# Norms of two halves of the tokens among the products, up weights in the ring's last words, and another fill at the recurrence's end

## The chip, the cores and the metric

The kernel runs on one core of a Trainium2 chip. The metric is the device time of one execution in microseconds (us), as the median of several runs. All data is fp32. A matmul instruction of the program is executed in fp32 as two passes, so that the trace counts 16 records where the program has 8 instructions. "PE" is the matmul engine, "PEld" its weight loads, DVE the vector engine, ACT the scalar engine, POOL the GpSimd engine, SP the engine that issues most transfers.

## The reference, cut to what matters

512 tokens of width 1024 are worked on: 256 of the context and 256 of the latent. Two blocks follow each other.

```
# first block: two layers
h = rmsnorm(x, norm_pre[i]) * (1 + scale) + shift          # both sequences
y = hgrn2_mixer(h) (i = 0) or mla_mixer(h) (i = 1)         # ends in @ w_out, 2048 -> 1024
x = x + gate * rmsnorm(y, norm_post[i])                    # layer 1: latent only
# second block: two layers
h = modulate(rms_norm(x, norm_mix[l]), sh1, sc1)
k, v, q, u, f, gt = split(h @ w_in[l])
x = x + g1 * merge_branches(attention, pool, fourier, gt) @ w_out
hf = modulate(rms_norm(x, norm_ffn[l]), sh2, sc2)
x = x + g2 * conv_ffn(hf, w_up[l], conv_w[l], w_down[l])
```

The context of the second block is a new input (`ctx_2`); its latent part is what the first block gives. The norm's mean goes over the width of one token, so the norm of one token never needs another token.

## The kernel before

Activations lie transposed: the width on the 128 partitions in 8 parts `k`, the tokens along the row, columns 0 to 255 the context (`CTX`), 256 to 511 the latent. `xT` is the stream, `hT` the normed input of a layer, `oz` the 16 heads of the recurrence, `ozm` those of the latent attention. All engines run programs written by hand and meet only at semaphores; the order on each engine is the order of the code.

**Weights** come through `ring_mem`, 12288 words for each partition, cut anew for each stage (`ring.stage`): slot `j` of a stage lies at `j * words`. SP runs one `ring.fill` after another in program order; before it loads a slot it waits until the last stage's user of these words (or of this slot's semaphore) is done (`strips_used`). `out{l}` has four slots of 2048 words, `up{l}` two slots of 2048 with 11 turns, `down{l}` four slots of 2816 words with two turns. So slots 0 and 1 of `up` (words 0 to 4095) lie where slots 0 and 1 of `down` (words 0 to 5631) will lie.

**A norm** (`norm_scalar`, `norm_tensor`, `norm_vector`) takes 8 squares on ACT, 8 matmuls with a matrix of ones that sum them over the partitions into a PSUM bank (L370), a root on ACT (L362), a reciprocal on DVE (L375), 8 products on DVE (L383), and where the layer modulates, 8 or 16 activations on ACT with scale and shift (L436, L444), which raise `h_ready` for the next matmuls. `post_vector` multiplies a mixer's output by the reciprocal (L1677) and adds it with its gate to `xT` (L1683).

**The recurrence** works on 8 pairs of heads (`PAIRS`). For a pair there are seven terms: PE forms scores (L703), DVE multiplies decays into `Kw`, `Qw`, `Tw` (L1622, L1624, L1629) and merges scores under a mask (L1627), ACT copies keys for the next term (L1344). After the last pair has been projected nothing but these terms is left, since pair 7 cannot overlap a pair 8. There the kernel puts matmuls of `hg_out` (L1279: heads `k` below `EARLY` = 14 of strips 0 and 1) among the terms, four after each of the first seven steps; the first of them waits until pair 6 has been read out by DVE (`hg_root_vector`, `hg_read_vector`, ending at L1670). For pair 7 DVE does both reciprocals and the readout of pair 6 right behind term 1.

**Then** `outer_tensor` (L781) forms the output product in 8 strips of 128 rows on all 512 columns, the norm `hg_post`, the norm `mla_pre` and the products of `mla_in_tensor` (L800, L807) follow each other, and `mla_z` (L816). After the attention pairs, `outer_tensor` forms `mla_out` for the latent, the norms `mla_post` and `mix0` follow, and then `in_tensor` (L955 keys, L962 values, L979 queries, L1001 the other inputs). The second block's later norms (`ffn0`, `mix1`, ...) are already done in two parts of the tokens, `_a` and `_b`, each beside products of the other.

## Time and profile before

| | us |
|---|---|
| median of 3 runs | 2774.67 |
| the 3 runs | 2774.24 to 2776.05 |
| the profiled execution | 2774.83 |
| its span, first to last instruction | 2773.0 |
| PE busy in the span | 2630.5 (95%) |
| DVE busy | 902.2 (33%) |
| ACT busy | 607.2 (22%) |

The profile comes from one execution. Busy time of PE includes matmuls at the lower clock; the time lost is therefore both in its waits and in stretches in which the granted clock is below 1. A row of the timeline gives start, duration, engine, line, operation, operands, the count of merged records and, in brackets, the idle time ahead and who ended it.

### The profile page before, as it was taken

What the parts mean: (1) busy time and instruction counts of PE and PEld (TensorE: products, weight loads), DVE (VectorE), ACT (ScalarE), POOL (GpSimd) and SP (SyncE); (2) the same over time, 40 slices, a digit from 0 to 9 for tenths busy, and PEclk for the clock granted to TensorE, in tenths of its full rate; (3) what the DMA queues carried; (4) which work ended last, traced back from release to release, by engine and by line L of the source; (5) the groups of instructions that cost most, each with busy time, mean ns of one, the idle gap of its engine ahead of it and who ended that gap; (6) DMA issues with size and microseconds to landing.
All of it is one profiled execution on the core that took longest, in us unless ns stands there. A gap on an engine that the chain in (4) does not pass through costs nothing.

```text
span 2773.0 us, 29216 instructions
## 1 busy us (share of the span) xinstructions
PE 2630.5 (95%) x11486; PEld 1715.6 (62%) x11486; DVE 902.2 (33%) x1503; ACT 607.2 (22%) x1072; POOL 52.9 (2%) x42
## 2 busy tenths in 40 slices
PE   7999999999997887899889999999998999999989
PEld 4566666666665434666746444774443587889878
DVE  2236446446446212244116101123232014113321
ACT  3112212212221112233114100122221013113321
POOL 0000000000000100000000000000000000000000
PEclk9999999999998998999989999999999999999999
DMA  8443333333340312212510121222224322253562
GB/s 319 163 137 130 127 136 128 129 136 127 130 133 4 114 30 91 59 38 71 137 46 16 49 72 61 76 61 76 76 76 114 83 51 87 87 156 107 152 181 76
DMA packets 319711, 280.21 MB, mean 101 GB/s; under 512 B 27617, under 2 KB 298601, under 8 KB 319513
## 3 DMA queue, kind: packets, MB, share of 16 engines
q1 hardware_dynamic: 317882, 274.89, 32.3%
q0 software_dynamic: 1280, 4.20, 0.4%
q8 instruction: 51, 0.84, 0.1%
q10 hardware_dynamic: 479, 0.13, 0.0%
q14 instruction: 19, 0.16, 0.0%
HBM read 278.15 MB, written 1.05 MB: 101 GB/s over the span
## 4 chain that ended last, share of the span: by engine, by line
PE 93%; DVE 3%; DMA 1%; ACT 1%; issue 1%; SPq 0%; ACTq 0%; DVEq 0%
PE ps L656 16%; PE ps L1176 15%; PE ps L1099 9%; PE ps L781 5%; PE ps L1192 4%; PE ps L1202 4%; PE ps L665 4%; PE ps L703 4%; PE ps L1135 3%; PE ps L1111 3%; PE ps L423 2%; PE ps L816 2%; PE ps L370 2%; PE ps L1001 1%; PE ps L979 1%; PE ps L1162 1%
## 5 line engine op out<-in xcount | busy, mean ns | idle before, releaser
L656 PE MATMUL ps<-hT,ring_mem 128*128 128x512 f32 x1024 | 455.9, 599 | 1.7 <-ACT hT L436 1.7
L1176 PE MATMUL ps<-hT,ring_mem 128*128 128x512 f32 (+1 forms) x1280 | 414.9, 487 | 2.6 <-DMA ring_mem<-in_w_up_dram 2.6
L1176 PEld LDWEIGHTS ps<-hT,ring_mem 128*128 128x128 f32 x1280 | 244.3, 191 | 172.4 <-issue 155.4
L656 PEld LDWEIGHTS ps<-hT,ring_mem 128*128 128x128 f32 x1024 | 191.3, 191 | 235.1 <-issue 232.4
L1099 PE MATMUL ps<-hT,ring_mem 128*128 128x512 f32 (+1 forms) x768 | 250.3, 486 | 0.0
L1099 PEld LDWEIGHTS ps<-hT,ring_mem 128*128 128x128 f32 x768 | 145.9, 190 | 101.3 <-issue 91.4
L1892 DVE SCALAR_TENSOR_TENSOR arena<-ps,vecs,arena 128x510 f32<-128x510 f32 (+1 forms) x176 | 100.3, 611 | 306.3 <-ACT arena L1498 299.9
L781 PE MATMUL ps<-arena,ring_mem 128*128 128x256 f32 (+1 forms) x456 | 144.6, 480 | 7.8 <-DVE arena L1670 7.8
L1192 PE MATMUL ps<-arena,ring_mem 128*128 128x512 f32 (+1 forms) x352 | 117.2, 496 | 14.4 <-DMA ring_mem<-in_w_down_dram 14.4
L703 PEld LDWEIGHTS ps<-arena,K_c 128*128 128x128 f32 x896 | 115.2, 192 | 23.6 <-issue 23.0
L781 PEld LDWEIGHTS ps<-arena,ring_mem 128*128 128x128 f32 x456 | 87.6, 192 | 64.5 <-issue 48.5
L1855 DVE TENSOR_TENSOR arena<-ps,arena 128x512 f32<-128x512 f32 (+1 forms) x48 | 26.8, 558 | 291.2 <-PE ps L1111 291.2
L703 PE MATMUL ps<-arena,K_c 128*128 128x128 f32 x896 | 117.8, 285 | 0.0
L1202 PE MATMUL ps<-arena,ring_mem 128*128 128x256 f32 (+1 forms) x704 | 116.1, 327 | 0.0
L665 PE MATMUL ps<-ring_mem,hT 128*128 128x256 f32 x512 | 113.0, 379 | 0.0
L1202 PEld LDWEIGHTS ps<-arena,ring_mem 128*128 128x128 f32 x704 | 106.5, 191 | 9.6 <-issue 0.5
L375 DVE RECIPROCAL rstd<-root 128x256 f32<-128x256 f32 (+2 forms) x15 | 31.1, 2073 | 240.0 <-ACT root L362 240.0
L1192 PEld LDWEIGHTS ps<-arena,ring_mem 128*128 128x128 f32 x352 | 68.5, 195 | 63.1 <-issue 42.5
L1864 DVE SCALAR_TENSOR_TENSOR xT<-ps,mod_b,xT 128x256 f32<-128x256 f32 (+1 forms) x60 | 23.8, 427 | 247.9 <-PE ps L1192 115.4
L1344 ACT ACTIVATE K_c<-arena 128x1024 f32<-128x1024 f32 x56 | 64.0, 1144 | 181.8 <-DVE arena L1624 159.3
L665 PEld LDWEIGHTS ps<-ring_mem,hT 128*128 128x128 f32 x512 | 96.1, 190 | 12.4
L357 ACT ACTIVATE hT<-xT 128x256 f32<-128x256 f32 (+2 forms) x88 | 34.5, 430 | 294.5 <-DVE xT L1864 264.9
(238 smaller groups left out, 2969.6 us busy)
## 6 DMA issues: line engine op xcount, KB each, us to landing
ring_mem<-in_w_mod_dram SPq DMA_DIRECT2D x24, 2048.0 KB, 7.7
ring_mem<-in_w_up_dram SPq DMA_DIRECT2D x88, 512.0 KB, 4.5
ring_mem<-in_hg_w_in_dram SPq DMA_DIRECT2D x40, 1024.0 KB, 5.1
ring_mem<-in_w_in_dram SPq DMA_DIRECT2D x30, 1024.0 KB, 5.4
ring_mem<-in_w_down_dram SPq DMA_DIRECT2D x16, 1408.0 KB, 7.2
ring_mem<-in_ada_w_dram SPq DMA_DIRECT2D x8, 2048.0 KB, 7.7
ring_mem<-in_mla_w_in_dram SPq DMA_DIRECT2D x9, 1024.0 KB, 5.4
ring_mem<-in_hg_w_out_dram SPq DMA_DIRECT2D x8, 1024.0 KB, 11.7
```

Source lines behind the costliest of these rows:

```text
L656: mm = PE.matmul(bank, wj[:, k, m * 128:m * 128 + 128], hT[:, k, :], start=k == 0, stop=k == 7)
L665: mm = PE.matmul(bank[:, g * 256:g * 256 + 256], hT[:, k, tok:tok + 128], wj[:, k, :], start=k == 0, stop=k == 7)
L703: mm = PE.matmul(dst, K_c[:, u * 128:u * 128 + 128], comb(Qw, 1 << (term - 1), u), start=True, stop=True)
L781: mm = PE.matmul(ps[:, j, 0:n], wj[:, k, :], src(k), start=k == 0, stop=k == kts - 1)
L1099: mm = PE.matmul(ps[:, j, 0:n], wj[:, k, m * 128:m * 128 + 128], hT[:, k, c0:T], start=k == 0, stop=k == 7)
L1111: mm = PE.matmul(ps[:, 3 + j, 0:n], wj[:, k, m * 128:m * 128 + 128], brT[:, k, c0:T], start=k == k0, stop=k == k1 - 1)
L1135: mm = PE.matmul(ps[:, (0 if part == "_a" else 4) + j, m * (hi - lo):(m + 1) * (hi - lo)], wj[:, k, m * 128:m * 128 + 128], yT[:, k, c0 + ...
L1176: mm = PE.matmul(ps[:, 2 * j + m, 0:n], wj[:, k, m * 128:m * 128 + 128], hT[:, k, c0:T], start=k == 0, stop=k == 7)
L1192: mm = PE.matmul(ps[:, 4 + j, 0:n], wj[:, k, :], hid[:, k, 0:n], start=k == 0, stop=k == FT - 1)
L1202: mm = PE.matmul(ps[:, (0 if part == "_a" else 4) + j, 0:hi - lo], wj[:, k, :], hid[:, k, lo:hi], start=k == 0, stop=k == FT - 1)
L1344: S.activation(view(K_c, (2 * h, PC // (2 * h)), (h, 2), (1, h)), comb(Kw, h), ACT.Copy).then_inc(kc_ready, 1)
L1892: ins = V.scalar_tensor_tensor(dst, src, tap(k, f, part), dst, ALU.mult, ALU.add)
```

## The change

Three things change.

- **Norms in two halves.** `hg_post`, `mla_pre` and `mix0` become `_a` (context) and `_b` (latent). The second four strips of `hg_out` are formed first for the context (`h == 0`, banks 4 to 7), then for the latent (banks 0 to 3); the context's post norm and pre norm are summed in the middle of the latter. The keys' weights are used first on the context while the latent's norms run, then the queries' weights, then the keys' weights on the latent. The norm of the new context (`mix0_a`) is summed during `mla_out`; `mla_post` and `mix0_b` are summed while `in0` works on the context. Squares go to other places (`y_sq`, `z_sq`), gates have their own `coef_post`, and each norm its own bank. `post_vector` alternates its two operations.
- **Ring.** `up{l}` gets slots 4 and 5 at words 8192 to 12287.
- **Recurrence's end.** 6 fill matmuls come ahead of the first scores (they need heads 0 to 11 only), then 4, 4, 4, 4, 2, 0, 2, 2, 0 behind the steps, and the 14 heads of strip 2 behind the last. DVE does the reciprocals of pair 6 behind terms 1 and 2 and its readout behind term 3.

```diff
-            ring.stage(f"up{l}", 2, 2048, FT // 2, [2] * 2)
+            ring.stage(f"up{l}", 2, 2048, FT // 2, [2] * 2, first_slot=4, at=8192)
...
+        def hg_close_tensor(pe, done, ready):
+            for j in range(4):
+                ring.wait_loaded(pe, "hg_out", j, 0)
+                k0 = done if j < 3 else 0
+                for k in range(k0, 16):
+                    if j == 0:
+                        ready(k)
+                    mm = PE.matmul(ps[:, j, :], strip("hg_out", j, 16)[:, k, :], oz[:, k, :], start=k == 0, stop=k == 15)
+                strip_used(mm)
+            for h in range(2):
+                for j in range(4):
+                    ring.wait_loaded(pe, "hg_out", j, 1)
+                    if h == 1:
+                        pe.wait_ge(y_kept, j + 1)
+                    for k in range(16):
+                        if h == 1 and j == 0 and k == 8:
+                            pe.wait_ge(y_kept, 5)
+                            norm_tensor(pe, "hg_post_a", lambda k: y_sq[:, k, 0:CTX], ones, CTX)
...
+                    if j == 2:
+                        pe.wait_ge(y_kept, 6)
+                        norm_tensor(pe, "mla_pre_a", lambda k: hT[:, k, 0:CTX], ones, CTX)
...
+        def mla_close_tensor(pe):
+            for t in range(2):
+                for j in range(4):
...
+                    if t == 1 and j == 0:
+                        pe.wait_ge(y_kept, 13)
+                        norm_tensor(pe, "mix0_a", lambda k: hT[:, k, 0:CTX], ones, CTX)
...
         def mla_in_tensor(pe):
...
+            pe.wait_ge(y_kept, 11)
+            keys(0, 0, CTX)
+            norm_tensor(pe, "hg_post_b", lambda k: y_sq[:, k, CTX:T], ones, LAT)
+            keys(1, 0, CTX)
+            pe.wait_ge(x_added, 10)
+            norm_tensor(pe, "mla_pre_b", lambda k: hT[:, k, CTX:T], ones, LAT)
             ring.wait_loaded(pe, "mla_a", 0, 0)
...
+            keys(0, CTX, T)
+            strip_used(keys(1, CTX, T))
...
             if l == 0:
-                keys("mix0", 0, T)
+                pe.wait_ge(y_kept, 20)
+                keys("mix0_a", 0, CTX)
+                norm_tensor(pe, "mla_post", lambda k: z_sq[:, k, :], ones, LAT)
+                values(0, 2)
+                queries(0, 0, CTX)
+                queries(1, 0, CTX)
+                norm_tensor(pe, "mix0_b", lambda k: hT[:, k, CTX:T], ones, LAT)
+                queries(2, 0, CTX)
+                queries(3, 0, CTX)
+                groups_in(3, 6, (0, 1)).then_inc(in_full, 1)
+                keys("mix0_b", CTX, T)
...
-            early = [(j, k) for j in range(2) for k in range(EARLY)]
-            for idx in range(10):
-                hg_core_after(pe, PAIRS - 1, idx)
...
+            early_out(6)
+            for idx, count in enumerate((4, 4, 4, 4, 2, 0, 2, 2, 0, EARLY)):
+                hg_core_after(pe, PAIRS - 1, idx)
+                early_out(count)
...
+        def hg_close_scalar(act):
+            for j in range(4):
+                wait_strip(act, "hg_out", j, 0)
+                S.activation(hT[:, j, :], ps[:, j, :], ACT.Copy).then_inc(y_kept, 1)
+            for h in range(2):
...
+                post_scalar(act, "hg_post" + part, [k + 1 + (4 * h if k >= 4 else 0) for k in range(8)], y_sq[:, :, cols], h * 256)
...
+                norm_scalar(act, "mla_pre" + part, src, lambda k: hT[:, k, cols], 256, at=h * 256)
+                modulate_part_scalar(act, "mla_pre", part, mod_a[1], cols, h)
...
+            for k in range(9):
+                if k < 8:
+                    V.tensor_tensor(hT[:, k, cols], hT[:, k, cols], rstd[:, cols], ALU.mult).then_inc(normed, 1)
+                if k:
+                    dve.wait_ge(normed, sq_base[name] + k)
+                    V.scalar_tensor_tensor(xT[:, k - 1, cols], hT[:, k - 1, cols], coef_post[:, k - 1, c:c + 1], xT[:, k - 1, cols],
+                                           ALU.mult, ALU.add).then_inc(x_added, 1)
...
-                    if gates and not first and term <= 2:
+                    if not first and term <= 2:
                         hg_root_vector(dve, i - 1, term - 1)
-                    if not gates and term == 1:
-                        for hd in range(2):
-                            hg_root_vector(dve, i - 1, hd)
-                    if not first and term == (3 if gates else 1):
+                    if not first and term == 3:
                         hg_read_vector(dve, st, i - 1)
```

**On PE at the recurrence's end, from the last pair's mean to the output product.** L700 and L703 are the scores of a term, L1279 the fill, L715 the turn of the keys, L727 the states. Before:

```order
L751 MATMUL ps<-arena,ones 128x512 x2
L700 MATMUL ps<-arena 128x128 x8
L703 MATMUL ps<-arena,K_c 128x128 x8
L1279 MATMUL ps<-arena,ring_mem 128x512 x4
L703 MATMUL ps<-arena,K_c 128x128 x8
...
L715 MATMUL ps<-ident,arena 128x128 x16
L727 MATMUL ps<-arena 128x128 x12
L745 MATMUL ps<-arena 128x128 x20
L751 MATMUL ps<-arena,ones 128x512 x2
L781 MATMUL ps<-arena,ring_mem 128x512 x36
```

After (scores L704 and L707, fill L1341, turn L719, output product L778 and L789):

```order
L755 MATMUL ps<-arena,ones 128x512 x2
L1341 MATMUL ps<-arena,ring_mem 128x512 x6
L704 MATMUL ps<-arena 128x128 x8
L707 MATMUL ps<-arena,K_c 128x128 x8
L1341 MATMUL ps<-arena,ring_mem 128x512 x4
...
L719 MATMUL ps<-ident,arena 128x128 x16
L1341 MATMUL ps<-arena,ring_mem 128x512 x2
L731 MATMUL ps<-arena 128x128 x12
L749 MATMUL ps<-arena 128x128 x20
L755 MATMUL ps<-arena,ones 128x512 x2
L1341 MATMUL ps<-arena,ring_mem 128x512 x14
L778 MATMUL ps<-arena,ring_mem 128x512 x22
```

Six fill matmuls stand ahead of the first scores and fourteen behind the mean, where before there was none; four that stood behind each late term are gone.

**On PE from the output product's end to the gates of the latent attention** (L370 the norms' sums, L800 the query inputs, L807 the keys and values, L816 the first gates). Before:

```order
L781 MATMUL ps<-arena,ring_mem 128x512 x64
...
L370 MATMUL ps<-arena,ones 128x512 x8
L370 MATMUL ps<-hT,ones 128x512 x8
L800 MATMUL ps<-hT,ring_mem 128x256 x16
L807 MATMUL ps<-hT,ring_mem 128x512 x16
...
L816 MATMUL ps<-hT,ring_mem 128x256 x16
```

After (L789 the output product, L374 the sums, L827 the keys, L841 the queries):

```order
L789 MATMUL ps<-arena,ring_mem 128x256 x72
L374 MATMUL ps<-arena,ones 128x256 x8
L789 MATMUL ps<-arena,ring_mem 128x256 x40
L374 MATMUL ps<-hT,ones 128x256 x8
L789 MATMUL ps<-arena,ring_mem 128x256 x16
L827 MATMUL ps<-hT,ring_mem 128x256 x8
L374 MATMUL ps<-arena,ones 128x256 x8
L827 MATMUL ps<-hT,ring_mem 128x256 x8
L374 MATMUL ps<-hT,ones 128x256 x8
L841 MATMUL ps<-hT,ring_mem 128x256 x16
L827 MATMUL ps<-hT,ring_mem 128x256 x16
```

The two norms of 512 columns in a row have become four of 256, three of which have products on the other half between them and the next.

**On PE from the last heads to the first rotations of the second block** (L955 keys, L962 values, L979 queries, L1001 inputs). Before:

```order
L781 MATMUL ps<-arena,ring_mem 128x256 x64
...
L370 MATMUL ps<-arena,ones 128x256 x8
L370 MATMUL ps<-hT,ones 128x512 x8
L955 MATMUL ps<-hT,ring_mem 128x512 x8
L962 MATMUL ps<-ring_mem,hT 128x128 x32
L979 MATMUL ps<-hT,ring_mem 128x512 x32
L1001 MATMUL ps<-ring_mem,hT 128x256 x32
```

After (L807 the product, L992 keys, L999 values, L1008 queries, L1021 inputs):

```order
L807 MATMUL ps<-arena,ring_mem 128x256 x80
L374 MATMUL ps<-hT,ones 128x256 x8
L807 MATMUL ps<-arena,ring_mem 128x256 x48
L992 MATMUL ps<-hT,ring_mem 128x256 x8
L374 MATMUL ps<-arena,ones 128x256 x8
L999 MATMUL ps<-ring_mem,hT 128x128 x16
L1008 MATMUL ps<-hT,ring_mem 128x256 x16
L374 MATMUL ps<-hT,ones 128x256 x8
L1008 MATMUL ps<-hT,ring_mem 128x256 x16
L1021 MATMUL ps<-ring_mem,hT 128x256 x16
L992 MATMUL ps<-hT,ring_mem 128x256 x8
```

The context's sum lies within the product, and products on the context lie behind each sum that the latent needs.

## Rows read from the trace of the kernel before

**Rows 1.** The page, chain that ended last, shares by engine.

```profile
PE 93%; DVE 3%; DMA 1%; ACT 1%; issue 1%; SPq 0%; ACTq 0%; DVEq 0%
```

**Rows 2.** PE's waits: line, released by, total us, times, longest us.

```profile
PE ps L370 <- ACT hT L357: 25.4, 2, 16.3
PE ps L1192 <- DMA ring_mem<-in_w_down_dram: 14.4, 2, 7.2
PE ps L1279 <- DVE arena L1670: 14.0, 1, 14.0
PE ps L800 <- ACT hT L436: 10.7, 2, 10.4
PE ps L781 <- DVE arena L1670: 7.8, 1, 7.8
```

**Rows 3.** Timeline, the recurrence's end.

```profile
851.75 3.48 PE L700 MATMUL ps<-arena 128*128 128x128 f32 x16 [5.49 <-DVE arena L1606]
...
862.41 3.35 DVE L1663 RECIPROCAL root<-root 128x512 f32<-128x512 f32 x1
...
884.45 1.23 DVE L1624 TENSOR_TENSOR arena<-arena 128x1024 f32<-128x1024 f32 x1 [0.48 <-PE ps L703]
...
885.59 1.35 DVE L1627 COPY_PREDICATED arena<-arena,ps 128x512 f32<-128x512 int32 x2
885.71 1.06 ACT L1344 ACTIVATE K_c<-arena 128x1024 f32<-128x1024 f32 x1 [4.16 <-DVE arena L1624]
...
887.68 1.95 PE L703 MATMUL ps<-arena,K_c 128*128 128x128 f32 x16
...
908.57 1.04 PE L715 MATMUL ps<-ident,arena 128*128 128x128 f32 x8
```

**Rows 4.** The chain in order of time, products: start, us, what, count.

```profile
930.51 89.19 PE ps L781 x200
...
1312.53 55.27 PE ps L781 x256
...
1419.11 27.47 PE ps L979 x64
```

**Rows 5.** Windows: length; busy us (count) of PE, PEld, DVE, ACT, POOL; granted clock; DMA share; GB/s.

```profile
1019.70:1089.00 69.30, 40.81 (x97) 19.79 (x98) 23.63 (x36) 18.47 (x35) 0.00 (x0) 0.78 0.05 15
...
1368.00:1412.00 44.00, 23.56 (x50) 11.40 (x51) 16.04 (x27) 17.52 (x36) 0.00 (x0) 0.73 0.15 48
...
2534.00:2536.00 2.00, 2.00 (x6) 1.61 (x7) 1.72 (x5) 0.42 (x1) 0.00 (x0) 0.54 1.09 320
```

**Rows 6.** Timeline, operations of 256 columns.

```profile
1377.67 3.25 DVE L1683 SCALAR_TENSOR_TENSOR xT<-hT,coef,xT 128x256 f32<-128x256 f32 x8
...
1795.12 1.75 DVE L375 RECIPROCAL rstd<-root 128x256 f32<-128x256 f32 x1 [9.99 <-ACT root L362]
1796.91 2.77 DVE L383 TENSOR_TENSOR hT<-xT,rstd 128x256 f32<-128x256 f32 x8
1797.43 4.04 ACT L444 ACTIVATE hT<-hT,mod_b,coef 128x256 f32<-128x256 f32 x8 [2.34 <-DVE hT L383]
```

**Rows 7.** Transfers: tensors, queue, count, size, median us from issue to landing.

```profile
ring_mem<-in_w_up_dram SPq DMA_DIRECT2D x88, 512.0 KB, 4.5
...
ring_mem<-in_w_down_dram SPq DMA_DIRECT2D x16, 1408.0 KB, 7.2
...
ring_mem<-in_hg_w_out_dram SPq DMA_DIRECT2D x8, 1024.0 KB, 11.7
```

**Rows 8.** Timeline: DVE's last hidden part (layer 0), SP's last up loads (layer 1).

```profile
2127.72 0.69 DVE L1901 TENSOR_TENSOR arena<-arena 128x512 f32 x1
...
2660.43 1.00 SPq L128 DMA_DIRECT2D ring_mem<-in_w_up_dram  x2
```

**Rows 9.** The chain in order of time, the down products.

```profile
2128.25 77.34 PE ps L1192 x176
...
2681.13 39.83 PE ps L1192 x176
```

More of the change, by code:

```diff
@@ new lines, in mla_close_tensor @@
+        def mla_close_tensor(pe):
+            for t in range(2):
+                for j in range(4):
+                    ring.wait_loaded(pe, "mla_out", j, t)
+                    if t == 1:
+                        pe.wait_ge(x_copied, KT + j + 1)
+                    for k in range(16):
+                        mm = PE.matmul(ps[:, 4 * t + j, 0:LAT], strip("mla_out", j, 16)[:, k, :], ozm[:, k, :], start=k == 0, stop=k == 15)
+                    strip_used(mm)
+                    if t == 1 and j == 0:
+                        pe.wait_ge(y_kept, 13)
+                        norm_tensor(pe, "mix0_a", lambda k: hT[:, k, 0:CTX], ones, CTX)
@@ L793, in mla_in_tensor, with keys @@
         def mla_in_tensor(pe):
+            ring.wait_loaded(pe, "mla_a", 1, 0)
+            wk_ = strip("mla_a", 1, 8)
+            def keys(m, lo, hi):
+                for k in range(8):
+                    if m == 0 and lo == 0:
+                        wait_h(pe, "mla_pre_a", k)
+                    mm = PE.matmul(ps[:, 1 + m, lo:hi], wk_[:, k, m * 128:m * 128 + 128], hT[:, k, lo:hi], start=k == 0, stop=k == 7)
+                return mm
+            pe.wait_ge(y_kept, 11)
[4 more added lines that the diff above has]
+            norm_tensor(pe, "mla_pre_b", lambda k: hT[:, k, CTX:T], ones, LAT)
             ring.wait_loaded(pe, "mla_a", 0, 0)
@@ L802, in mla_in_tensor @@
             strip_used(mm)
-            ring.wait_loaded(pe, "mla_a", 1, 0)
-            wj = strip("mla_a", 1, 8)
-            for m in range(2):
-                for k in range(8):
-                    mm = PE.matmul(ps[:, 1 + m, :], wj[:, k, m * 128:m * 128 + 128], hT[:, k, :], start=k == 0, stop=k == 7)
-            strip_used(mm)
+            keys(0, CTX, T)
+            strip_used(keys(1, CTX, T))
             with pe.Fori(0, 2) as t:
@@ L978, in in_tensor @@
+            mm.then_inc(rot_full, 1)
+            ring.wait_loaded(pe, name, 4, 0)
+            ws = strip(name, 4, 8)
+            for n_g, g in enumerate(groups):
                 for k in range(8):
-                    mm = PE.matmul(ps[:, 2 + j, 0:n], wj[:, k, (j % 2) * 128:(j % 2) * 128 + 128], hT[:, k, c0:T],
+                    mm = PE.matmul(ps[:, n_g // 2, (n_g % 2) * 256:(n_g % 2) * 256 + 256], hT[:, k, g * 128:g * 128 + 128], ws[:, k, :],
                                    start=k == 0, stop=k == 7)
-                if j % 2:
-                    strip_used(mm)
-                else:
+                if n_g == 1 and l == 0:
@@ new lines, in mla_close_scalar, with keep, ctx2, src @@
+        def mla_close_scalar(act):
+            def keep(t):
+                for j in range(4):
+                    wait_strip(act, "mla_out", j, t)
+                    S.activation(hT[:, 4 * t + j, CTX:T], ps[:, 4 * t + j, 0:LAT], ACT.Copy).then_inc(y_kept, 1)
+            keep(0)
+            def ctx2(k):
+                act.wait_ge(x_copied, KT + k // 2 + 1)
+                return xT[:, k, 0:CTX]
+            norm_scalar(act, "mix0_a", ctx2, lambda k: hT[:, k, 0:CTX], CTX)
+            modulate_part_scalar(act, "mix0", "_a", mod_b[0][:, 0:8, :], slice(0, CTX), 0)
+            keep(1)
+            post_scalar(act, "mla_post", [12 + k + 1 for k in range(8)], z_sq, CTX)
+            def src(k):
+                act.wait_ge(x_added, 16 + k + 1)
+                return xT[:, k, CTX:T]
+            norm_scalar(act, "mix0_b", src, lambda k: hT[:, k, CTX:T], LAT, at=CTX)
+            modulate_part_scalar(act, "mix0", "_b", mod_b[0][:, 0:8, :], slice(CTX, T), 1)
```

240 lines of the change are left out of this document (119 added, 121 removed).

## The prediction, made before the changed kernel had run

> **What bounds the kernel now.** I read the chain that ended last first: 93% of the span lies on PE [rows 1]. So work moved between other engines is worth nothing by itself; a gain must come out of the time in which PE waits or runs at the lower clock. The list of PE's waits names those the change touches: 25.4 us before norm sums (16.3 in the first block's end, the rest at the second block's start), 14.4 for down weights in two waits of 7.2, 14.0 for the readout of pair 6, 10.7 for the first modulated part and 7.8 for the readout of pair 7 [rows 2]. Then the windows: the 69.3 us between the output product and the gates hold 97 matmul passes at a granted clock of 0.78, and the 44.0 us behind `mla_out` hold 50 at 0.73 [rows 5]. What a pass costs at full clock comes from long products: 27.47 / 64 = 0.429 us for 512 columns and 55.27 / 256 = 0.216 for 256 [rows 4]. Halving the columns thus costs nearly nothing (2 x 0.216 - 0.429 = 0.003 us a pair; some 290 passes are halved, 0.8 us, which the sums with 0.216 contain). A step over `k` is two passes: 0.858 or 0.432.
>
> **Part A, the recurrence's end.** The window of interest runs from the first scores, 851.75, to the output product's end, 930.51 + 89.19 = 1019.70 [rows 3, 4]. Six fill steps take 6 x 0.858 = 5.1 us and just fit into the wait of 5.5 ahead of the scores [rows 3]; PE then starts them at full clock, where the row shows 3.48 for 16 passes against 1.95 later. That brings DVE's first term some 1.3 us forward. From there the terms are paced by DVE or by a ring of three engines. With nothing else on DVE a term takes: multiply 1.23, key copy on ACT 1.06, scores on PE 1.95, and handovers of some 0.4 (an estimate): 4.7 us. With a reciprocal (3.35) or the readout (four operations of 512 columns at about 0.69 [rows 8], 2.8) between, DVE alone takes 1.23 + 1.23 + 1.35 [rows 3] + the decays' product (1.2 falling to 0.6, an estimate from its width, halved each term) + that. From the first term's multiply, some 5 us behind the scores' start at 856.7 (an estimate), I get steps of 9.2 (its own columns are interleaved and slow), 8.2 and 7.2, then three of 4.7, then 1.2 to the end of the last multiply: 896.5 for the turn of the keys, against 908.57 [rows 3]: 12.1 us. The reason is that the four fill steps (3.4 us) now lie beside DVE's reciprocals and no longer in front of each late term's scores, and that nobody waits for pair 6. Two fill steps between turn and states give back 1.1 of it (1.7, less a short wait for ACT that is there anyway): 11.0.
>
> Behind the mean PE waited 7.8 for pair 7 [rows 2]. Now 14 fill steps stand there, 12.0 us, longer than DVE's two reciprocals and readout, so 7.8 go. In both kernels 28 of 128 steps are done by the mean, so 100 remain: at full clock 85.8, where the row has 89.2 [rows 4]: 3.4 more. Sum 22.2. Against it stands the clock. While DVE paces the terms PE will have gaps of 1 to 2.7 us. A gap of 2.6 us ahead of the second up turn of layer 1 was followed by 2 us at a mean 0.54, the 1.2 GHz level for most of it [rows 5]. Scores at half clock are only on the path in the last three terms, 1 us each; I take 1 in all and up to 5 as the bound. **A = 21** (bounds 10 and 24).
>
> The second load of strip 0 is now issued at about 925 and wanted at about 942 (14 fill steps, closing of three strips at 1.7, then 13.7 for strip 3). A load of `hg_out` landed in 11.7 us in the median, twice the others of its size, while POOL fetches its tables from the readout of pair 7 on [rows 7]. So it should land some 3 us early. The Trainium skill, "DMA: Bandwidth & Descriptors", section "Issuing engines are not separate DMA queues", says that transfers of all queues run on the same 16 engines and interleave; three strips are now asked for inside that burst instead of two, and by that rule the first could be late. If its landing grew by half of 11.7, PE would wait some 3 us; this is no term of the sum, and the lower bound of A covers it.
>
> **Part B, two norms in halves.** Pure work of the old window: 64 passes of 512 and 32 of 256, 64 x 0.429 + 32 x 0.216 = 34.4 of 69.3 us, 34.9 lost [rows 5]. What is lost after:
> - Context. Its post norm is summed inside the latent's first strip; root, reciprocal 1.75, then eight pairs at 0.35 + 0.41 (2.77 / 8 and 3.25 / 8 [rows 6]), 6.4, some 10 us in all, against 17.2 of products. No wait. From the sum of `mla_pre_a` to its last modulated part: root 0.7, 1.75, 0.5, 4.04 [rows 6] = 7.0, beside 6.9 of strip 3. Behind it ACT must still copy three strips that PE waits for, an estimated 0.4 each and 0.1 for the modulated part's end: 1.4 us.
> - Latent. After `hg_post_b` 0.7 + 1.75 + 6.4 + a square = 9.8 with its own sum, and PE has one product of 3.5 and the sum's 3.5 to put beside it: 2.9 lost. Then from the sum to the first modulated part 3.5, and a pace of 0.5 a step set by ACT (4.04 / 8) over PE's 0.43: 0.6. So 4.1.
> - Clock. PE is half idle over some 15 us here; cold starts cost 1.5 (3.48 against 1.95 [rows 3]) to 3.4 (part A) each before. I take 3.5 (bounds 0 and 7).
>
> Lost 1.4 + 2.9 + 4.1 + 3.5 = 11.9. **B = 23** (bounds 17 and 27). `mla_z`'s first strip reuses the slot of the query inputs; it has 6.9 us of key products to arrive in, where it had 13.7. Loads of this size without company take about 5.4 (double the 512 KB at 4.5 is an upper end, 9.0 [rows 7]): nothing, at worst 2, since the other slots follow in the same rhythm as before.
>
> **Part C, the second block's start.** Behind the last strip, 1368.00, to 1412.00 PE's pure work is 16 x 0.216 + 32 x 0.429 = 17.2 and two passes of the next product; 26.5 of 44.0 are lost [rows 5]. After: `mix0_a` is summed behind strip 4, with three strips (20.7 us) for its 7 us chain. `mla_post` is summed behind a key product, and three pieces (values, an estimated 3.6, two queries 6.9) cover its 9.8 us chain. `mix0_b` is followed by two queries and two input groups, 13.8 us, over a chain of 7. Left is a wait of 0.5 for ACT's last copy. SP has asked for each `in0` slot as soon as the strip before it in its words is done; the tightest, strip 3, has 28 us. **C = 26** (bounds 23 and 27). The product and inputs lose their cold starts with it, already counted.
>
> **Part D, down weights.** Slots 0 and 1 of `down` lay over both slots of `up`, so their load began when `up` ended, and 1408 KB land in 7.2 us [rows 7]: twice 7.2 of wait [rows 2]. With `up` at words 8192 on they overlap `out`, long done, and SP issues them behind the last `up` load, at 2660.43 in layer 1, 13.5 us before the products want them [rows 8]. They lie behind 1 MB of `up`, 5 + 6 = 11 us in sum; in layer 0 there is twice the time. Slots 2 and 3 wait for `up`'s end but are wanted 19 and 28 us later (22 steps of 0.43 a strip). What is late next is the hidden layer: its last part was done at 2127.72 + 0.69, when the chain shows the product starting at 2128.25 [rows 8, 9]. It now starts at 2121.1, but reaches `k` = 21 only 18 us later; in layer 1 the distance is 9. No wait. The two products lose a cold start: 77.3 - 176 x 0.429 = 1.8 and 39.8 - 176 x 0.216 = 1.8 [rows 9]. **D = 18** (bounds 14 and 19). The wait of 2.6 for `up`'s second turn in layer 1 stays, since slot 0 is still loaded again only when its first use ends.
>
> **Sum.** 21 + 23 + 26 + 18 = 88 us. The profiled execution took 2774.83, 1.8 more than its span and 0.2 over the median. 2773 - 88 + 1.8 = **2687 us**.
>
> **Rivals.**
> 1. *The recurrence is bound by DVE, and the fill moves without gain.* For it: DVE's total is unchanged. Against: DVE waited for PE's scores in each late term, and 14.0 us of PE's wait is for pair 6 only. A would keep the 7.8, the 3.4 and little else: 11, time 2697. Chance 0.10.
> 2. *The clock.* The gaps at the recurrence's end and in part B keep PE at 1.2 GHz through them and into the products: twice 5 us more: 2697 to 2700. The rows of before show recovery within a few us of steady work. Chance 0.10.
> 3. *The down weights don't come early*, because in-order SP is held at something ahead of them or they collide with the last `up` loads: D is 0 to 5, 2700 to 2705. Chance 0.05.
> 4. *Slower.* The up weights in their new place arrive late in each turn: in layer 1 a slot has 6.9 us from its last use to its next and the two loads need about 5.2 (4.5 in the median, the second half a us later [rows 7]). Were they each 6 us slower, 20 turns would wait 4.4 us, 88, and the gain would be gone; from there on it is slower. Nothing in the trace makes a place in SBUF slow. Chance 0.03, time 2775 and above.
>
> **How the numbers follow.** Forecast 0.72, range of its own 2678 to 2695; the rivals as above. Some wait that I don't see (a strip, a bank) is worth 5 to 10 us anywhere in B or C, and DVE's pace in A could come out better. I take 2673 to 2703, which leaves out the slower case and parts of 2 and 3. Faster by over 0.2% (which is about what a measurement of this kernel tells from no change): 0.96. Within 0.2%: 0.01. Slower: 0.03.
>
> **What would show it.** The turn of the keys near 896; no wait for a readout above 1 us; the gates starting near 1045 (1089 less A and B); `mix0`'s sums without waits and the rotations some 26 us closer to the end of the heads; both waits for down weights gone, and the product's start at the up product's end. Wrong would be: a DMA wait in the output product, scores paced at more than 5 us in the last three terms, or a granted clock below 0.9 from 870 to 1000.

## The result, and the profile after

| | median us | runs | lowest and highest |
|---|---|---|---|
| before | 2774.84 | 4 | 2774.24 to 2776.05 |
| after | 2684.03 | 4 | 2681.87 to 2685.21 |

The ratio is 0.9671 with a 95% interval of 0.9655 to 0.9688: the kernel is 90.8 us faster, and the forecast of 2687 lies 3 us above the time. The profiled execution has a span of 2682.0 us, 91.0 less than before.

The chain that ended last, by engine, and PE's waits (line, released by, total us, times, longest us), to be read beside [rows 1, 2]:

```profile
PE 95%; DVE 2%; DMA 1%; ACT 1%; SPq 0%; issue 0%; ACTq 0%; DVEq 0%
...
PE ps L707 <- ACT K_c L1405: 9.0, 5, 2.4
...
PE ps L841 <- ACT hT L448: 3.6, 1, 3.6
...
PE ps L1235 <- DMA ring_mem<-in_w_up_dram: 2.5, 1, 2.5
...
PE ps L827 <- issue: 0.9, 1, 0.9
PE ps L374 <- DVE xT L1775: 0.8, 1, 0.8
```

All five rows of [rows 2] are gone, 72.3 us in sum. With them went a sixth of the kernel before, ahead of the keys of the second block, which the prediction's list leaves out and which lies in part C:

```profile
PE ps L955 <- ACT hT L436: 10.4, 1, 10.4
```

Small waits took their place: 9.0 in the recurrence's terms, 3.6 ahead of the query inputs of the latent half, and three of under 1 us. In all PE's idle time fell from 142.5 us (span 2773.0 less 2630.5 busy) to 66.2 (2682.0 less 2615.8), that is by 76.3. The other 14.7 of the 91.0 went out of PE's busy time, which holds the cold starts behind the waits, that is, matmuls that run at 1.2 GHz until the clock rises.

The chain in order of time (start, us, what, count) for parts A and B (the recurrence's end and the two norms in halves), to be read beside [rows 4]:

```profile
912.23 12.02 PE ps L1341 x28
924.25 18.88 PE ps L778 x44
...
994.93 3.45 PE ps L374 x16
998.38 6.91 PE ps L789 x32
...
1026.42 9.90 PE ps L841 x32
1036.33 6.91 PE ps L827 x32
1043.23 27.64 PE ps L853 x128
```

From the mean (912.23) to the end of the output product, PE has no gap: both sums of the context (L374, one at 974.21 and this one at 994.93) lie inside the product at 0.216 us a pass. The product's end without these two sums (2 x 3.45) is 998.38 + 6.91 - 6.90 = 998.4, against 1019.70. The gates (L853) start at 1043.23; in the kernel before they start at 1089.14.

### The profile page after: what moved, and what is told of

The parts are those of the page before. It is cut to its first block, busy times and chain, and to the rows that moved or that the text cites. A ratio compares the mean times of both kernels' runs of the same rounds, so it can differ in the third digit from the quotient of the medians.

```text
span 2682.0 us, 29803 instructions
## 1 busy us (share of the span) xinstructions
PE 2615.8 (98%) x11774; PEld 1764.1 (66%) x11774; DVE 904.6 (34%) x1530; ACT 613.0 (23%) x1103; POOL 53.0 (2%) x42
## 4 chain that ended last, share of the span: by engine, by line
PE 95%; DVE 2%; DMA 1%; ACT 1%; SPq 0%; issue 0%; ACTq 0%; DVEq 0%
PE ps L660 17%; PE ps L1235 15%; PE ps L1158 9%; PE ps L1261 4%; PE ps L1251 4%; PE ps L669 4%; PE ps L707 4%; PE ps L1194 3%; PE ps L1170 3%; PE ps L427 2%; PE ps L853 2%; PE ps L807 2%; PE ps L789 2%; PE ps L374 2%; PE ps L1008 2%; PE ps L1221 1%
## 5 line engine op out<-in xcount | busy, mean ns | idle before, releaser
L1235 PE MATMUL ps<-hT,ring_mem 128*128 128x512 f32 (+1 forms) x1280 | 413.2, 486 | 2.5 <-DMA ring_mem<-in_w_up_dram 2.5
L1235 PEld LDWEIGHTS ps<-hT,ring_mem 128*128 128x128 f32 x1280 | 243.1, 190 | 171.8 <-issue 155.3
L707 PEld LDWEIGHTS ps<-arena,K_c 128*128 128x128 f32 x896 | 116.2, 194 | 34.3 <-issue 20.1
L707 PE MATMUL ps<-arena,K_c 128*128 128x128 f32 x896 | 120.1, 289 | 9.1 <-ACT K_c L1405 9.0
L1261 PE MATMUL ps<-arena,ring_mem 128*128 128x256 f32 (+1 forms) x704 | 116.1, 327 | 0.0
L1251 PE MATMUL ps<-arena,ring_mem 128*128 128x512 f32 (+1 forms) x352 | 113.8, 486 | 0.0
L1261 PEld LDWEIGHTS ps<-arena,ring_mem 128*128 128x128 f32 x704 | 106.5, 191 | 9.6 <-issue 0.5
L1251 PEld LDWEIGHTS ps<-arena,ring_mem 128*128 128x128 f32 x352 | 66.9, 190 | 46.6 <-issue 42.1
L1717 DVE TENSOR_TENSOR arena<-arena 128x1024 f32<-128x1024 f32 x56 | 76.4, 1365 | 54.8 <-PE ps L707 54.6
L1170 PE MATMUL ps<-arena,ring_mem 128*128 128x512 f32 (+1 forms) x256 | 85.2, 486 | 0.0
```

The costliest lines, as they stand in the source:

```text
L707: mm = PE.matmul(dst, K_c[:, u * 128:u * 128 + 128], comb(Qw, 1 << (term - 1), u), start=True, stop=True)
L1170: mm = PE.matmul(ps[:, 3 + j, 0:n], wj[:, k, m * 128:m * 128 + 128], brT[:, k, c0:T], start=k == k0, stop=k == k1 - 1)
L1235: mm = PE.matmul(ps[:, 2 * j + m, 0:n], wj[:, k, m * 128:m * 128 + 128], hT[:, k, c0:T], start=k == 0, stop=k == 7)
L1251: mm = PE.matmul(ps[:, 4 + j, 0:n], wj[:, k, :], hid[:, k, 0:n], start=k == 0, stop=k == FT - 1)
L1261: mm = PE.matmul(ps[:, (0 if part == "_a" else 4) + j, 0:hi - lo], wj[:, k, :], hid[:, k, lo:hi], start=k == 0, stop=k == FT - 1)
L1717: V.tensor_tensor(comb(Qw, h), comb(Qw, h), view(Tw, (2 * h, n), (PC - h, 2), (0, h), at=h), ALU.mult).then_inc(merged, 1)
```

## Where the 91 us went

Differences of the two traces, at the borders that the prediction used:

| part | read at | measured | predicted |
|---|---|---|---|
| A | product's end, 1019.70 to 998.4 | 21.3 | 21 |
| B | gates' start, 1089.14 to 1043.23, less A | 24.6 | 23 |
| C | last heads to first rotations, 147.9 to 121.9 | 26.0 | 26 |
| D | two waits and two cold starts | 18.0 | 18 |
| not predicted | the up product of layer 1 | 1.7 | 0 |

The sum is 91.6; 0.5 is given back in the heads of the latent attention, a stretch (gates' start to the product behind the heads) of 223.4 us before and 223.9 after, and of 223.3 in a second trace of the changed kernel. Another 0.5 lies ahead of the changed places: the last unpacking of the recurrence (L745 before, L749 after) starts at 839.98 before and 840.46 after. Counted from there A is 21.8.

**A.** The timeline of PE at the recurrence's end (start, us, engine, line, operation, count, in brackets the idle time ahead and its releaser), and the window over the last scores, to be read beside [rows 3]:

```profile
852.18 2.05 PE L704 MATMUL ps<-arena 128*128 128x128 f32 x16 [0.29 <-DVE arena L1699]
...
883.13 2.05 PE L707 MATMUL ps<-arena,K_c 128*128 128x128 f32 x16 [1.44 <-ACT K_c L1405]
...
892.05 3.67 PE L707 MATMUL ps<-arena,K_c 128*128 128x128 f32 x16 [2.41 <-ACT K_c L1405]
895.56 1.88 PE L1341 MATMUL ps<-arena,ring_mem 128*128 128x512 f32 x4
897.28 1.04 PE L719 MATMUL ps<-ident,arena 128*128 128x128 f32 x8
```

```profile
892.00:894.00 2.00, 1.95 (x9) 1.95 (x10) 1.48 (x3) 0.00 (x0) 0.00 (x0) 0.52 0.00 0
```

The first scores start without the wait of 5.5 and at full clock (2.05 us, not 3.48). DVE's key products of the seven terms (L1717) start at 857.14, 866.03, 873.86, 880.77, 885.22, 889.68 and 895.76, that is 8.9, 7.8, 6.9, then 4.5, 4.5 and 6.1 apart. The last term has no fill behind the step before it (its count is 0), so PE idled 2.41 us, and its scores ran at a granted clock of 0.52.

**B.** 44.8 us from the product's end to the gates, where 34.4 are pure work; 10.4 are lost. The window from 1005.30, and the first six microseconds of the query inputs (columns as in [rows 5]):

```profile
1005.30:1043.30 38.00, 32.55 (x130) 25.89 (x131) 12.93 (x28) 11.80 (x30) 0.00 (x0) 0.91 0.10 28
1026.00:1032.00 6.00, 5.58 (x13) 4.53 (x14) 1.93 (x6) 3.72 (x8) 0.00 (x0) 0.50 0.00 0
```

PE waited 3.60 for the first modulated part of the latent half (L841, the query inputs) and then worked for almost 6 us at 1.2 GHz: 9.90 us for 32 passes that cost 6.91 at full clock.

**C.** The chain behind the last heads:

```profile
1325.82 0.52 issue
1326.34 3.69 PE ps L992 x16
...
1388.98 0.43 PE ps L1049 x2
```

`mix0_a` (1301.65) lies within the product, `mla_post` and `mix0_b` between inputs of the context. There is one gap, 0.52 us, ahead of the keys of the context. The chain calls it "issue"; in the timeline ACT's copy of the last strip (L1461) runs until 1326.24, 0.1 ahead of the keys. The product itself starts at 1267.11 (1312.53 before), and the first rotation stands at 1388.98, 121.9 behind it; before, it stood at 1460.39, 147.9 behind.

**D and the up product.** The chain at both down products (L1251) and at the up product of layer 1 from its second turn on (L1235), and SP's queue, where the down loads now stand directly behind the last up load:

```profile
2049.62 75.53 PE ps L1251 x176
...
2453.32 138.40 PE ps L1235 x640
2591.71 37.99 PE ps L1251 x176
```

```profile
2023.61 26.41 SPq L128 DMA_DIRECT2D ring_mem<-in_w_down_dram  x4
...
2579.43 15.70 SPq L128 DMA_DIRECT2D ring_mem<-in_w_down_dram  x4
```

The products took 75.53 and 37.99 us, against 77.34 and 39.83 in [rows 9], and start where the up product ends: two waits of 7.2 and twice 1.8. The loads were issued 26 and 12 us before they were wanted. The 1.7 us come from the up product of layer 1, 138.40 against 140.10 before; runs 8 to 12 come back to it.

## The experiments

The theory is that the gain is what the sum says: at four places PE's wait, and the cold start behind it, are filled with other work, and the four add up since no place feeds another. There are three rivals. The parts overlap, so that one edit would have got most of it. Or the fill's place at the recurrence's end is free and only DVE's order counts. Or what is left in A and B is the clock and not a dependence.

Each of the first four ran in three rounds beside the kernel before, 2774.92 there.

**1. The ring alone**, in the kernel before (the ring's helper also learns the two new arguments):

```diff
-            ring.stage(f"up{l}", 2, 2048, FT // 2, [2] * 2)
+            ring.stage(f"up{l}", 2, 2048, FT // 2, [2] * 2, first_slot=4, at=8192)
```

> The kernel before with the up weights in the ring's last words and nothing else. Theory (the parts are independent): both waits for down weights (7.2 each) go and each down product loses its cold start (1.8 each), so 18 us, 2775 to 2757. Rival (a part's gain shows only beside the others, or is given back by the loads colliding): 0 to 10 us.

Measured 2756.19 (2754.15 to 2757.17), ratio 0.9931 (0.9915 to 0.9948), 18.7 us less. The chain of its trace has the down products as short as after:

```profile
2121.09 75.53 PE ps L1192 x176
```

The two waits are gone from its list of PE's waits, and nothing is late next: the up product's end is the start of the down product. In this trace the two places are worth 18.0 together and the up product of layer 1 is 1.7 shorter (138.40); the medians' 18.7 lies 1.0 below that sum, within the spread of the runs. Rivals 3 and 4 of the prediction fall.

**2. The recurrence's end alone**, in the kernel before (the fill's order and DVE's order; the output product and the norms stay whole):

```diff
-            early = [(j, k) for j in range(2) for k in range(EARLY)]
-            for idx in range(10):
-                hg_core_after(pe, PAIRS - 1, idx)
...
+            early_out(6)
+            for idx, count in enumerate((4, 4, 4, 4, 2, 0, 2, 2, 0, EARLY)):
+                hg_core_after(pe, PAIRS - 1, idx)
+                early_out(count)
```

> The kernel before with the new fill and the new DVE order at the recurrence's end and nothing else (strip 2 closed from head 14 on as well). Theory: the turn of the keys moves from 56.9 to some 45.2 us behind the end of the last unpacking, the waits for readouts (14.0 and 7.8) go, 21 to 22 us, 2753. Rival (the time comes back before the norms, since the second load of strip 0 is asked for inside the burst of table loads): a DMA wait of 3 us or more in the output product and 15 to 18 us of gain.

Measured 2752.94 (2752.0 to 2753.67), ratio 0.992 (0.9903 to 0.9936), 22.0 us less. In its trace the gates start at 1066.67, 22.5 earlier than before (21.5 if counted from the last unpacking, which starts 1.0 earlier in this trace).

```profile
PE ps L1192 <- DMA ring_mem<-in_w_down_dram: 14.3, 2, 7.2
...
PE ps L703 <- ACT K_c L1352: 7.4, 5, 2.4
```

These are two of PE's waits. Those of parts B (25.4 and 10.6) and D stand in the list unchanged, those for the readouts have gone. Rival 1 (A worth 11) falls.

**3. The norms alone**: the changed kernel with the old recurrence's end and `up` in its old words (both diffs above, reversed).

> The changed kernel with the recurrence's end and the ring of before, so that only the norms in halves are left. Theory: 24.6 us between the output product's end and the gates and 26 at the second block's start, 50 us, 2724 to 2725. Rival (the halves gain less without the long product stretch of the new fill ahead of them): under 45.

Measured 2725.53 (2723.55 to 2727.7), ratio 0.9819 (0.9802 to 0.9835), 49.4 us less. The gates start at 1066.05, 23.1 earlier than before. From the last unpacking, which this trace reaches 1.5 later, it is 24.6, and from the product behind the heads to the first rotation (1289.57 to 1411.43) it is 26.0 less than before: both parts are as large as in the changed kernel. The down products took 78.41 and 40.40 here, 1.6 more than before in sum, which may be why 49.4 is less than 24.6 + 26.0. Of PE's waits, those of D and A are back, while B's stay as in the changed kernel (3.6 ahead of L841):

```profile
PE ps L1251 <- DMA ring_mem<-in_w_down_dram: 14.5, 2, 7.3
PE ps L1338 <- DVE arena L1755: 14.0, 1, 14.0
```

Three parts alone give 18.7 + 22.0 + 49.4 = 90.1, the whole 90.8. They add up to within the spread of the runs, and the rival that they overlap falls. B and C had no run each to itself; they are told apart by the two places in this trace.

**4. DVE's old order** in the changed kernel: both reciprocals behind the first term, the readout with it, the fill as after.

```diff
-                    if not first and term <= 2:
+                    if gates and not first and term <= 2:
                         hg_root_vector(dve, i - 1, term - 1)
-                    if not first and term == 3:
+                    if not gates and term == 1:
+                        for hd in range(2):
+                            hg_root_vector(dve, i - 1, hd)
+                    if not first and term == (3 if gates else 1):
```

> The changed kernel with DVE's old order at the recurrence's end (both reciprocals and the readout of pair 6 behind term 1), fill unchanged. Theory: the third term's scores wait for 9.5 us of DVE work with only 3.4 of fill beside it, PE goes cold, but DVE's work in sum is the same, so the turn of the keys comes 4 us later (2 to 7): 2688. Rival (only where the fill stands matters): turn at the same place within 1 us.

Measured 2687.24 (2686.79 to 2687.7), 3.2 above the changed kernel. The third scores waited for all of DVE's block at once and then ran cold:

```profile
873.90 3.78 PE L707 MATMUL ps<-arena,K_c 128*128 128x128 f32 x16 [8.07 <-ACT K_c L1405]
```

The turn of the keys came 3.05 later (L719 at 900.33 against 897.28), or 3.5 if both are counted from the last unpacking; 4 was expected. Spreading DVE's work over three terms is thus worth some 3 us of A's 21; it lets the fill steps, which are spread too, stand beside it.

The next four ran in five rounds beside the kernel before, 2775.45 there.

**5. The fill spread evenly**, DVE's new order kept:

```diff
-            early_out(6)
-            for idx, count in enumerate((4, 4, 4, 4, 2, 0, 2, 2, 0, EARLY)):
+            for idx, count in enumerate((4, 4, 4, 4, 4, 4, 4, 0, 0, 0)):
```

> The changed kernel with the fill of the recurrence's end spread evenly: no fill step ahead of the first scores, four behind each of the first seven steps of the core (28 in all, two strips), none behind the mean, and strip 2 not begun early; DVE keeps its new order. Theory that the place of the fill matters by itself: the wait of 5.5 ahead of the first scores returns (3.5 to 5.5 us of it on the path), and behind the mean PE waits again for the readout, at least the 7.8 of before less what DVE's new order saves, plus the cold start of the product behind it (3.4): 12 to 15 us above the changed kernel. Rival, that DVE's order alone made the gain and the fill's place is free: 0 to 3 us above it.

Measured 2696.64 (2695.26 to 2697.98), ratio 0.9718 (0.9704 to 0.9731): 12.6 above the changed kernel's 2684.03, or 12.0 if each is compared with the kernel before that ran beside it. On PE:

```profile
853.73 3.46 PE L704 MATMUL ps<-arena 128*128 128x128 f32 x16 [5.49 <-DVE arena L1698]
...
901.65 1.04 PE L719 MATMUL ps<-ident,arena 128*128 128x128 f32 x8
...
923.68 2.90 PE L778 MATMUL ps<-arena,ring_mem 128*128 128x512 f32 x3 [7.85 <-DVE arena L1762]
```

The size is as the theory has it, the split is not. This trace entered the pair 1.5 us later than that of the changed kernel (L749 at 841.97 against 840.46), and so did its first scores (853.73 against 852.18): DVE releases them at the same time, with or without work ahead of them. I had expected 3.5 to 5.5 of that wait on the path, and none of it is. The six steps ahead are worth 1.2 by the clock of the first scores, and more by not being elsewhere. Counted from L749, the turn comes 2.9 later: 1.2 for that cold start and 1.6 for two late terms, which four fill steps each stretch to 5.2 us from 4.5. From the turn on it is 0.8 less for two steps fewer, 7.85 for the readout of pair 7 that nothing covers, and 2.6 for the cold start behind it (33.49 for 72 passes that took 12.02 + 18.88). Sum 12.5. The rival falls: the same 28 steps stand ahead of the mean in both, and where they stand, and that 14 steps of strip 2 cover the readout behind it, is worth 12.6. Most of that is the uncovered readout (7.85 and the cold start of 2.6).

**6. Two steps moved** from between turn and states to behind step 5, where the last scores had gone cold:

```diff
-            for idx, count in enumerate((4, 4, 4, 4, 2, 0, 2, 2, 0, EARLY)):
+            for idx, count in enumerate((4, 4, 4, 4, 2, 2, 2, 0, 0, EARLY)):
```

> The changed kernel with two fill steps taken from between the turn of the keys and the states and put behind step 5, where its trace has none and the last scores ran at half clock (3.67 us for 16 passes against some 2.05). Nothing is computed more or less. Theory (steady work keeps the clock, and the two steps behind the turn lie on the path): 1.6 for the scores and 1.1 for the two steps, 2.7 us below the changed kernel. Rival, that DVE sets the pace there or ACT's wait behind the turn takes the place of the steps: 0 to 1 below it.

Measured 2679.38 (2678.63 to 2682.62), ratio 0.9655 (0.9642 to 0.9669), 4.7 below 2684.03 where 2.7 was expected; the trace shows less of it. PE's timeline:

```profile
893.46 2.05 PE L707 MATMUL ps<-arena,K_c 128*128 128x128 f32 x16 [0.69 <-ACT K_c L1405]
```

The last scores take 2.05 after a gap of 0.69. From L749 at 841.89 to the first step behind the mean at 911.25 it is 69.4 us, against 71.8 in the changed kernel: 2.4, of which 1.6 to the turn. The two steps behind the turn were worth 0.8 and not 1.1, since ACT's wait ahead of the states (0.69) shows up in their place. That is a gain in a place where PE's wait was "for ACT": the wait itself was harmless, the clock behind it not.

**7. Work in the gap of part B**: eight matmuls of ones into a bank that is free there, ahead of the query inputs. Their result isn't used.

```diff
             norm_tensor(pe, "mla_pre_b", lambda k: hT[:, k, CTX:T], ones, LAT)
+            pe.wait_ge(y_kept, 12)
+            for k in range(8):
+                PE.matmul(ps[:, 3, 0:CTX], ones, hT[:, k, 0:CTX], start=k == 0, stop=k == 7)
```

> The changed kernel with eight matmuls more, of the ones with parts of the hidden state into an unused bank, in the wait of 3.6 us ahead of the second group of context keys (the first work on the second half's modulated parts). They stand for work that keeps PE busy; nothing reads their result. In the changed kernel the 32 passes behind that wait took 9.90 us, against 6.9 at full clock. Theory, that half of this is the clock: 1.5 to 2.5 us below the changed kernel. Rival, that ACT's pace of one part in 0.5 us sets it: no change, or up to 0.5 slower.

Measured 2681.46 (2680.14 to 2683.16), ratio 0.9662 (0.9648 to 0.9675), 2.6 below 2684.03. One line of its chain:

```profile
1028.22 7.50 PE ps L844 x32
```

(L844 is L841 of the changed kernel, three lines down.) 2.4 us less than 9.90, at a granted clock of 1.00; the 0.6 above 6.91 are put down to ACT's pace of a part in 0.5 us (eight parts in 4.04 us). So of the 3.0 lost in that group 2.4 were clock.

**8. Both.**

> Both edits of the two runs before together: the two fill steps behind step 5, and the eight matmuls of ones in the wait ahead of the second group of context keys. They lie 60 us apart and share no wait, so by the theory they add: 4 to 5 us below the changed kernel. Were both rivals right, no difference from it.

Measured 2680.61 (2680.44 to 2682.91), ratio 0.966 (0.9647 to 0.9673): 3.4 below 2684.03 where 4 to 5 were expected, and no better than the moved steps alone. Its trace holds both gains (from L749 to the first step behind the mean 69.4, 7.50 for L844), so something else took them back. Part of it is in the up product of layer 1, which took 140.00 us in this trace and 138.40 in the three before.

**9 to 12. The changed kernel and runs 6 to 8 once more**, side by side in five rounds; before 2774.07 there.

> The changed kernel as it is, run beside the next three on one chip, so that differences of 2 to 5 us between them can be read. Expected where it was, 2684, within 2.

> The two fill steps behind step 5, again. Its trace had the first step of the output product 2.4 us nearer to the core's start than in the changed kernel, so 2.4 us below the changed kernel of this call; if that is given back later, 0 to 1.

> The eight extra matmuls of ones ahead of the second group of context keys, again. Its trace had the 32 passes there in 7.50 us against 9.90, so 2.4 us below the changed kernel of this call; if given back later, 0 to 1.

> Both edits, again. Its trace had both gains (2.4 and 2.4 us), then gave 0.6 back behind the latent's heads and 1.6 in the up product of layer 1, which ran its start at half clock there and not in the other traces. If this last is chance from run to run, the medians lie 3 to 4.5 us below the changed kernel of this call; if it comes with the edits, 2 to 3.

| kernel | median us | lowest and highest | ratio to before, interval |
|---|---|---|---|
| after | 2683.1 | 2682.15 to 2684.98 | 0.9672 (0.9659 to 0.9685) |
| two steps moved | 2681.72 | 2679.23 to 2682.34 | 0.9664 (0.9651 to 0.9678) |
| work in the gap | 2682.73 | 2680.35 to 2684.16 | 0.9669 (0.9656 to 0.9682) |
| both | 2680.32 | 2677.82 to 2681.83 | 0.966 (0.9647 to 0.9673) |

The traces tell more than the medians. The chain of the changed kernel's second trace has the two places again:

```profile
1027.74 8.57 PE ps L841 x32
...
2452.93 140.08 PE ps L1235 x640
```

The same kernel, the same wait ahead of the first place (3.59 us, 3.60 in the first trace), and another time: 8.57 where the first trace had 9.90. The second place took 140.08 where it had 138.40, behind a wait of 2.69 us where the first trace had 2.53. And the kernel with only the steps moved, whose part B is untouched, had 9.75 in its first trace and in its second

```profile
1025.27 7.50 PE ps L841 x32
```

as if the gap were filled. So the cold start behind the gap of part B comes and goes from one execution to the next. Over all traces: without the extra matmuls the 32 passes took 9.90, 9.85, 9.75, 8.83, 8.83, 8.57 and 7.50 us, with them 7.50 four times. The up product of layer 1 took 138.40 in six traces (one of them with the ring change alone) and 139.9 to 140.1 in eight. All three kernels with the old ring are among the eight (140.10 each), but so are five of the eleven traces with the new one; whether the ring has a part in it, these traces can't tell.

What follows: moving the steps gains 2.4 us in each of the four traces that have it (69.3 to 69.4 us from L749 to the first step behind the mean, against 71.8 in the four without), the extra matmuls 0 to 2.4 and 1.5 on average (the mean of the seven is 9.0). Both together lie 2.8 below the changed kernel in the median, and their slowest run (2681.83) is below its fastest (2682.15) beside them. That is 0.10%, less than the 0.2% that a comparison with the kernel before can tell, and the move alone (1.4) and the extra work alone (0.4) are not separated from nothing by the medians. Expected were 2.4, 2.4 and, for both, 3 to 4.5: all three came out smaller, and what took the rest is not known. So the rival that what is left in A and B is the clock is true in part: 1.6 of it in A in every trace, and 0 to 2.4 in B; the rest of B's loss is waits.

## Why the prediction was right, point by point

**What bounds the kernel.** Right. The gain was time in which PE had waited (76.3) or run at half clock, and it appeared in full, since nothing else became late. The list of waits in the prediction was not complete (10.4 us ahead of L955 is missing), but the sum for C was taken from the window of 44.0 us and holds it.

**A, predicted 21, measured 21.3.** The steps of the terms, predicted 9.2, 8.2, 7.2 and three of 4.7, in sum 38.7, were 8.9, 7.8, 6.9, 4.5, 4.5 and 6.1, in sum 38.6; each is 0.2 to 0.4 shorter than the working had it, and the last is longer by its cold scores, the 1 us of clock that stood as a term of its own. The turn came at 897.28 (896.5, or 897.5 with that term), which is 11.3 earlier where 12.1 was forecast; 0.5 of the difference is the later start of the whole stretch. Behind the turn I had 7.8 + 3.4 - 1.1 = 10.1; it was 111.1 - 101.1 = 10.0. No wait for a readout is left. One reason was only half right: the six steps ahead of the scores bring the first term forward by the clock (1.3 predicted, 1.2 by run 5), but they also cost nothing there, which makes room in the late terms. Run 4 confirms the other reason, DVE's reciprocals no longer in one piece, with 3.2 of the 21.

**The second load of strip 0 of `hg_out`.** It was issued at 925.99, predicted 925. The four second loads landed in 12.8 us in the median and 14.8 at most (9.8 and 14.0 before), and PE has no wait for any of them: the second strips begin at 943.13, 17 us behind the issue. So the margin was there. It was larger than the "some 3 us" of the prediction: its own numbers, 942 - 925 - 11.7, give 5.3. Strip 0 itself landed 12.9 us after its issue, 4.2 ahead of its use. By the rule of the Trainium skill named in the prediction ("DMA: Bandwidth & Descriptors", "Issuing engines are not separate DMA queues") transfers of all queues interleave on the same engines. The median grew by 3.0 us, which agrees with it in sign; the slowest grew by 0.8, and the growth stayed within the margin.

**B, predicted 23, measured 24.6.** Of the 11.9 predicted lost, 10.4 were. Context 0.89 (1.4 predicted). Latent sum: a wait of 0.82 and 1.8 of pace in the sum, 2.6 (2.9). The eight pairs of DVE operations in front of it, taken as 6.4 though 8 x (0.35 + 0.41) is 6.1, took 5.9. From the sum to the first part 3.6 (3.5), pace 0.6 (0.6) as run 7 shows. Clock 2.4 and 0.2 for short cold starts (3.5). So the clock was the term that I had too large, by 1; and the later traces show that it isn't one number but anything between 0 and 2.4, without an edit that explains it. That the forecast of B came near is in this part luck: the second trace of the changed kernel would have given 1.3 more, the second one with the steps moved 2.4 more.

**C, predicted 26, measured 26.0.** One wait of 0.52 where 0.5 was forecast, and the cause is the one named, ACT's last copy.

**D, predicted 18, measured 18.0**, and 18.0 in the trace of run 1 too. The wait of 2.5 for the second turn of `up` in layer 1 stayed, as forecast. I took its cold start to stay as well. It had gone in the first trace after, for 1.7 us; since it is back in the second one, that is no lasting effect of the change.

**Rivals.** The clock never cost 10 us: from 870 to 1000 the granted clock was 0.99. What it cost stood behind two gaps, of 2.41 and of 3.60 us, and was 1.6 and 2.4. DVE's bound (rival 1) and the ring's (3 and 4) fell with runs 1 and 2.

The forecast was 3 us too high: 0.3 in A, 1.6 in B and 1.7 in the up product, less the 0.5 given back in the heads.

## What to carry to other kernels

When PE is 93% of the chain, list its waits and give each the independent work that is nearest in the program: halves of the tokens for norms, later products for the end of a recurrence, words of the ring whose last user is long done for weights. The price of a wait is the wait and the cold start behind it, and fill goes where the chain waits, not evenly: where it stood was worth 12 us here, with the same 128 steps of the product in both kernels. Gaps of 0.7 and 1.4 us in the terms were never followed by the low clock here, gaps of 2.1 us and more often were, so two steps of fill in a gap of 2.4 gained 1.6. Parts that fill different waits add up, so each can be tried alone.

## What the runs showed of the hardware

The clock behind a gap is not determined by the gap's length alone. A wait of 3.6 us ahead of the same 32 matmuls was followed by 6 us at 0.50, 0.75 or 1.00 of full speed in three traces (two of the same kernel, one with an edit 130 us earlier). The windows, of the changed kernel's second trace and of the second trace with the steps moved (the first is above):

```profile
1027.70:1033.70 6.00, 5.96 (x21) 5.08 (x22) 1.55 (x5) 3.34 (x7) 0.00 (x0) 0.75 0.00 0
```

```profile
1025.30:1031.30 6.00, 6.00 (x26) 4.41 (x27) 1.47 (x5) 3.26 (x7) 0.00 (x0) 1.00 0.00 0
```

In the recurrence's terms the same scores (16 passes, 2.05 us at full clock) stand behind gaps of several lengths. Behind 0.7 or 1.4 us they always took 2.05. The gap of some 2.1 us ahead of the third scores was followed by 2.05 in two traces (the changed kernel's first and that with the even fill) and by 3.25 to 3.68 in eight; behind 2.34 and 2.36 they took 2.05. The gap of 2.41 ahead of the last scores was followed by 3.06 to 3.67 in all six traces that have it. The low clock of the third scores cost the path nothing, because the next scores then waited 0.7 instead of 2.3 for ACT's copy; that of the last scores cost 1.6.

The wait of the up product in layer 1 was 2.48 to 2.59 us in the six traces with 138.40 and 2.52 to 2.78 in the eight with 140. All five waits above 2.6 were followed by the low clock, and of the eight between 2.52 and 2.59 three. In the changed kernel's second trace (2.69 us) the granted clock was still 1.00 in the first microsecond of the product and 0.50 from its second on, so it fell while PE was at work again.

I had expected that a gap costs its cold start or does not. What decides it, no run here shows, and it stays open. The Trainium skill, "TensorE: Matmul & The Clock Gate", Part 1, says that the unit which watches TensorE's activity runs free and isn't reset when the kernel starts, so that the same kernel differs from run to run in how many of its first matmuls are cold. It says so of a kernel's start; the traces here show the like in the middle of one, with 9.90 and 8.57 us for the same passes of the same kernel. Whoever compares kernels has to reckon with single traces that differ by 1 to 2 us at each such place, and has to read a gain of that size at the place itself and in more than one trace.
